# Hymba trunk layer on eight cores: order of loads and of the q, k, v projections at the start of the program

## The reference, cut to what matters

```python
h    = RMSNorm_pre(x)
p    = h @ W_in + b_in            # (16384, 2048) @ (2048, 5376)
q, k, v, g_attn, glu_val, glu_gate, g_conv = split(p)
attn = SlidingWindowGQA_with_sinks(partial_rope(q), partial_rope(k), v) * silu(g_attn)
conv = ConformerConv(glu_val, glu_gate) * silu(g_conv)
x    = x + RMSNorm_post(concat([attn, conv]) @ W_out + b_out)
```

## Time and profile before

| | us |
|---|---|
| median of 3 runs | 1105.92 (1105.06 to 1109.22) |
| the profiled execution | 1108.99 |
| its span, slowest core (core 2) | 1107.5 |
| spans of all cores | 1089.4 to 1107.5 |
| PE busy, core 2 | 1034.8 (93%) |
| DVE, ACT, POOL busy | 531.1 (48%), 412.2 (37%), 212.8 (19%) |
| DMA moved, core 2 | 141.92 MB |

### The profile page before, as it was taken

The page is one execution under the profiler, slowest core; times in us unless marked ns, Lnnn a source line. Parts: engine busy times, 40 slices in busy tenths (PEclk is TensorE's granted clock), DMA queues, the critical chain, the costliest instruction groups (busy, mean ns, idle before and its releaser), DMA issues.

```text
span 1107.5 us, 17820 instructions; the slowest of 8 cores (1089.4 to 1107.5 us)
## 1 busy us (share of the span) xinstructions
PE 1034.8 (93%) x6848; PEld 543.7 (49%) x6906; DVE 531.1 (48%) x921; ACT 412.2 (37%) x1013; POOL 212.8 (19%) x215
## 2 busy tenths in 40 slices
PE   3799999899999999999999999989999999999996
PEld 1556444555555444445544644455655544444443
DVE  3566301466665355446636650045776636533434
ACT  2452112556555445034511212155565544402111
POOL 0260000134543320000000000012455341000000
PEclk9899999999999999999999999999999999999999
DMA  8874334655566589979499303344645657992445
GB/s 184 277 113 79 57 48 76 127 116 117 128 136 131 147 191 159 192 200 204 91 171 185 78 10 67 76 102 108 177 122 140 152 141 174 165 180 41 81 76 109
DMA packets 26533, 141.92 MB, mean 128 GB/s; under 512 B 5985, under 2 KB 6369, under 8 KB 15969
## 3 DMA queue, kind: packets, MB, share of 16 engines
q0 software_dynamic: 8784, 80.74, 43.1%
q1 hardware_dynamic: 17666, 60.04, 17.7%
HBM read 171.72 MB, written 32.51 MB: 184 GB/s over the span
## 4 chain that ended last, share of the span: by engine, by line
PE 73%; DMA 7%; SPq 6%; DVE 6%; ACT 3%; issue 3%; POOL 1%; ACTq 0%; DVEq 0%; POOLq 0%
PE psum L1144 19%; PE psum L775 10%; PE psum L1023 10%; SPq L152 6%; DMA arena<-arena 5%; PE psum L635 5%; PE psum L1113 5%; PE psum L869 4%; PE psum L818 4%; PE psum L828 4%; PE psum L631 3%; PE psum L593 2%; ACT arena L928 2%; PE psum L530 1%; PE psum L1182 1%
## 5 line engine op out<-in xcount | busy, mean ns | idle before, releaser
L1144 PE MATMUL psum<-arena 128*128 128x512 bf16 x939 | 207.2, 379 | 1.1
L1144 PEld LDWEIGHTS psum<-arena 128*128 128x128 bf16 x960 | 93.6, 98 | 111.3
L818 PE MATMUL psum<-arena 128*128 128x352 bf16 (+1 forms) x768 | 124.3, 316 | 0.0
L828 PE MATMUL psum<-arena 128*128 128x352 bf16 (+1 forms) x768 | 120.9, 311 | 3.4 <-ACT arena L831 3.3
L928 ACT ACTIVATE arena<-psum,arena 128x128 f32<-128x128 f32 x256 | 93.9, 367 | 61.4 <-DVE arena L918 43.6
L1023 PE MATMUL psum<-arena 128*128 128x512 bf16 x500 | 110.9, 379 | 4.3 <-ACT arena L1027 3.0
L775 PE MATMUL psum<-arena 128*128 128x512 bf16 x502 | 113.6, 387 | 0.5
L828 PEld LDWEIGHTS psum<-arena 128*128 128x128 bf16 x768 | 74.8, 98 | 42.9 <-issue 5.3
L818 PEld LDWEIGHTS psum<-arena 128*128 128x128 bf16 x768 | 72.5, 99 | 47.6 <-issue 12.7
L907 DVE COPY_PREDICATED psum<-arena,psum 128x1024 f32<-128x1024 uint16 x32 | 38.7, 1208 | 117.7 <-PE psum L901 117.7
L942 POOL TENSOR_TENSOR arena<-arena 128x1024 bf16<-128x1024 f32 x32 | 60.5, 1892 | 140.7 <-DVE arena L941 140.7
(11 more groups left out here) (129 smaller groups left out, 1282.9 us busy)
## 6 DMA issues: line engine op xcount, KB each, us to landing
arena<-w_in POOLq DMA_DIRECT2D x12, 2048.0 KB, 16.0
arena<-x_ext SPq DMA_DIRECT2D x18, 1024.0 KB, 10.6
arena<-w_in POOLq DMA_DIRECT2D x16, 1024.0 KB, 10.4
out<-arena POOLq DMA_DIRECT2D x15, 1024.0 KB, 9.2
arena<-w_out POOLq DMA_DIRECT2D x6, 2048.0 KB, 20.2
arena<-arena SPq DMA_DIRECT2D x64, 66.0 KB, 2.0
arena<-arena SPq DMA_DIRECT2D x64, 65.9 KB, 2.0
arena<-arena SPq DMA_DIRECT2D x64, 65.9 KB, 2.3
```

Of the source, the lines that this page charges most:

```text
L818: cx.op('pe', lambda e, k=k: e.matmul(out=bank[bv][:, 0:n], lhsT=wbuf.ap[:, k, o:o + 128], rhs=xv[:, k, st:st + n], start=(k == 0), stop=( ...
L828: cx.op('pe', lambda e, k=k: e.matmul(out=bank[bg][:, 0:n], lhsT=wbuf.ap[:, k, o + 128:o + 256], rhs=xv[:, k, st:st + n], start=(k == 0), ...
L1144: cx.op('pe', lambda e, k=k: e.matmul(out=bank[b], lhsT=MIX.ap[:, k, j * 128:(j + 1) * 128], rhs=wo[n][k][0].ap[:, wo[n][k][1], :], start= ...
```

## The change

The program's first part is reordered; no arithmetic is changed.

- SP loads x tiles 0, 1, 2, the k/v bias and x tile 3 without a wait. POOL waits for x tile 1, then loads the k/v weights in two halves of 0.5 MB (as written) and the four quarters of q. x tile 4 waits for the second k/v half, tiles 5 to 7 for q's second, third and fourth quarter and for their buffer.
- The rotary tables are computed on DVE ahead of the copies of the norm's weights; the two sines on ACT come behind `p1_sq` of tile 2. A root is taken on ACT at the very start.
- Tiles 0 to 3 are projected by weight: k/v of all four, then q's first half (QA), then its second half (QB). Tiles 4 to 7 are projected tile by tile, k/v and q; tile 8, k/v alone.
- A product waits for the half of the transposed tile that it reads. k's rotation has scratch buffers of its own.

```diff
--- before.py
+++ after.py
@@ -367,6 +367,7 @@
         s_kvw = cx.dsem("kvw")
+        s_kvw2 = cx.dsem("kvw2")
...
@@ -410,7 +411,7 @@
-        rr_u = mk(O_CV + 2048, [NTIL, 8], F32)
+        rr_us = [mk(O_CV + o_, [NTIL, 8], F32) for o_ in (2048, 5120)]
...
             for which in range(2):
+                rr_u = rr_us[which]
...
-                cx.op('act', lambda e, which=which: e.activation(
+
+        def rope_sin():
+            for which in range(2):
+                rr_u = rr_us[which]
+                cx.op('act', lambda e, which=which, rr_u=rr_u: e.activation(
                     out=cs.ap[:, :, which * 8:(which + 1) * 8], in_=rr_u.ap, func=AF.Sin,
...
+            def xh(j, k):
+                return xts[j].a if k < 8 else xts[j].b
...
+            rk1 = [at([2, 2, 8], F32) for _ in range(2)]
+            rk2 = [at([2, 2, 8], F32) for _ in range(2)]
...
+                kvh = [mk(O_Z + 4096 * h, [8, 256], BF16) for h in range(2)]
...
-                kf, kb, r1, r2 = kvf[n % 3], kb2[n % 3], rt1[n % 2], rt2[n % 2]
+                kf, kb, r1, r2 = kvf[n % 3], kb2[n % 3], rk1[n % 2], rk2[n % 2]
...
-                        start=(k == 0), stop=(k == 15)), R=[KVW, xts[j]], W=[BK[b]])
+                        start=(k == 0), stop=(k == 15)), R=[kvh[k // 8], xh(j, k)], W=[BK[b]])
...
@@ -668,86 +682,87 @@
             if s == 0:
                 bufs = p1_bufs(0)
                 gp = bufs[2]
-                order = [1, 2, 3, 4, 5, 6, 7, 8, 0]
                 grow = mk(O_AT, [D], F32)
                 wslot["n"] = 1
                 wq0 = [[mk(O_WB + h * 8192 + q * 4096, [8, 256], BF16) for q in range(2)] for h in range(2)]
+                wq0f = wq0[0] + wq0[1]
                 cx.dma('sp', grow.ap[0:1, :], gpre_d[0:1, :], s_gpre, W=[grow], nowait=True)
                 cx.dma('sp', pos_i.ap, pos_t, s_c2, W=[pos_i], nowait=True)
                 cx.dma('sp', cpa.ap, cpack_d[:, 0:NCA], s_c, W=[cpa], nowait=True)
-                p1_load(0, order[0], 0, bufs)
+                order = [1, 2, 3, 4, 5, 6, 7, 8, 0]
+                for n in range(3):
+                    p1_load(0, order[n], n, bufs)
+                cx.dma('sp', bkv.ap, bqkv_d[:, 1024:1280], s_bkv, W=[bkv])
+                p1_load(0, order[3], 3, bufs)
+                for h, sem in ((0, s_kvw), (1, s_kvw2)):
+                    cx.dma('pool', kvh[h].ap, wv(w_in, 1024, 256, 8 * h, 8), sem, R=[bufs[0][1]], W=[kvh[h]])
                 for i in range(4):
-                    cx.dma('pool', wq0[i // 2][i % 2].ap, wv(w_in, 256 * (i // 2), 256, 8 * (i % 2), 8), s_wq[i],
-                           R=[cpa], W=[wq0[i // 2][i % 2]])
-                p1_load(0, order[1], 1, bufs, R=[wq0[0][0]])
-                cx.dma('sp', bq.ap, bqkv_d[:, 0:1024], s_bqkv, R=[wq0[0][1]], W=[bq])
-                p1_load(0, order[2], 2, bufs)
-                p1_load(0, order[3], 3, bufs, R=[wq0[1][0]])
-                p1_load(0, order[4], 4, bufs, R=[wq0[1][1]])
-                cx.dma('sp', cpb_.ap, cpack_d[:, NCA:NCP], s_c3, W=[cpb_])
-                cx.dma('sp', bkv.ap, bqkv_d[:, 1024:1280], s_bkv, W=[bkv])
+                    cx.dma('pool', wq0f[i].ap, wv(w_in, 256 * (i // 2), 256, 8 * (i % 2), 8), s_wq[i], W=[wq0f[i]])
+                p1_load(0, order[4], 4, bufs, R=[kvh[1]])
+                cx.dma('sp', bq.ap, bqkv_d[:, 0:1024], s_bqkv, W=[bq])
                 onesr = mk(O_AT + 8192, [128], F32)
                 cx.op('dve', lambda e: e.memset(onesr.ap, 1.0), W=[onesr])
+                cx.op('act', lambda e: e.activation(out=smp[3].ap[:, 0:1], in_=onesr.ap[:, 0:1], func=AF.Sqrt),
+                      R=[onesr], W=[smp[3]])
                 cx.op('dve', lambda e: e.tensor_copy(out=idn.ap, in_=cp[:, C_ID:C_ID + 128]), R=[cpa], W=[idn])
                 gpq = [mk(gp.off + n * 2048, [512], F32) for n in range(4)]
                 for n in range(4):
                     cx.op('pe', lambda e, n=n: e.matmul(
                         out=bank[n], lhsT=onesr.ap[0:1, :], rhs=grow.ap[0:1, n * 512:(n + 1) * 512],
                         start=True, stop=True), R=[onesr, grow], W=[BK[n]])
+                rope_tables()
+                for n in range(4):
                     cx.op('dve', lambda e, n=n: e.tensor_copy(
                         out=gpq[n].ap, in_=bank[n]), R=[BK[n]], W=[gpq[n]])
-                rot["i"] = 4
+                rot["list"] = [0, 1, 2, 3]
+                rot["i"] = 0
                 junk = mk(O_AT + 12288, [D], BF16)
-                xns = {}
-                rope_tables()
-
-                def qstep(n, done=None):
-                    j = order[n]
-                    b_ = q_a(0, j, wq0, done, 'pool')
-                    return lambda: q_b(0, j, b_)
-
-                p1_sq(0, order[0], 0, bufs, junk)
-                xns[0] = p1_n(0, order[0], 0, bufs)
-                p1_b(0, order[0], xns[0])
-                p1_sq(0, order[1], 1, bufs, junk)
-                xns[1] = p1_n(0, order[1], 1, bufs)
-                b0, b1 = nbank(), nbank()
-                q_h(b0, order[0], wq0, 0)
-                p1_b(0, order[1], xns[1])
-                p1_sq(0, order[2], 2, bufs, junk)
-                for n in (5, 6):
-                    p1_load(0, order[n], n, bufs)
-                q_h(b1, order[1], wq0, 0)
-                q_h(b0, order[0], wq0, 1)
-                f0 = qstep(0, b0)
-                xns[2] = p1_n(0, order[2], 2, bufs)
-                p1_sq(0, order[3], 3, bufs, junk)
-                later(f0)
-                q_h(b1, order[1], wq0, 1)
-                f1 = qstep(1, b1)
-                p1_b(0, order[2], xns[2])
-                xns[3] = p1_n(0, order[3], 3, bufs)
-                p1_load(0, order[7], 7, bufs)
-                p1_load(0, order[8], 8, bufs)
-                p1_sq(0, order[4], 4, bufs, junk)
-                later(f1)
-                for n in range(2, 9):
-                    if n + 1 < 9:
-                        p1_b(0, order[n + 1], xns[n + 1])
-                    if n + 2 < 9:
-                        xns[n + 2] = p1_n(0, order[n + 2], n + 2, bufs)
-                    fq = qstep(n) if order[n] > 0 else None
-                    if n + 3 < 9:
-                        p1_sq(0, order[n + 3], n + 3, bufs, junk)
-                    if fq:
-                        later(fq)
-                    if n == 3:
-                        cx.dma('pool', KVW.ap, wv(w_in, 1024, 256), s_kvw, W=[KVW])
-                        wq1 = wload(w_in, 512)
+                xns, kvs, qs = {}, {}, {}
+
+                def SQ(n):
+                    p1_sq(0, order[n], n, bufs, junk)
+
+                def N(n):
+                    xns[n] = p1_n(0, order[n], n, bufs)
+                    if n + 5 < 9:
+                        p1_load(0, order[n + 5], n + 5, bufs, R=[wq0f[n + 1]] if n < 3 else ())
+
+                def B(n):
+                    p1_b(0, order[n], xns[n])
+
+                def KV(n):
+                    kvs[n] = kv_a(order[n])
+
+                def KT(n):
+                    kv_b(order[n], kvs[n])
+
+                def QA(n):
+                    q_h(4 + n, order[n], wq0, 0)
+
+                def QB(n):
+                    q_h(4 + n, order[n], wq0, 1)
+                    qs[n] = q_a(0, order[n], wq0, 4 + n, 'pool')
+
+                def QQ(n):
+                    qs[n] = q_a(0, order[n], wq0, None, 'pool')
+
+                def QT(n):
+                    q_b(0, order[n], qs[n])
+
+                SQ(0), N(0), B(0), SQ(1), N(1), B(1), SQ(2), rope_sin(), N(2)
+                KV(0), B(2), SQ(3), N(3), KV(1), KT(0), B(3), KV(2), KT(1), KV(3), KT(2)
+                QA(0), QA(1), QA(2), QA(3), KT(3), SQ(4), N(4)
+                QB(0), B(4), KV(4), QB(1), SQ(5), N(5), B(5), QT(0), QB(2), KT(4), KV(5)
+                QT(1), QB(3), SQ(6), N(6), B(6), QT(2)
+                rot["list"] = list(range(8))
+                QQ(4), KT(5), KV(6), SQ(7), N(7), B(7), QT(3)
+                cx.dma('sp', cpb_.ap, cpack_d[:, NCA:NCP], s_c3, W=[cpb_])
+                wq1 = wload(w_in, 512)
+                QQ(5), KT(6), KV(7), SQ(8), N(8), B(8), QT(4)
+                QQ(6), KT(7), KV(8), QT(5), QQ(7), KT(8)
                 late_consts()
-                for jj in order:
-                    kb = kv_a(jj)
-                    later(lambda jj=jj, kb=kb: kv_b(jj, kb))
+                later(lambda: QT(6))
+                later(lambda: QT(7))
             else:
                 wq0, wq1 = nxt["wq"]
                 for j in range(1, 9):
```

More of the change, by code:

```diff
@@ L425, in rope_tables @@
             for which in range(2):
+                rr_u = rr_us[which]
                 shift = 0.25 if which == 0 else 0.0
                 lo, hi = (-1.5 * PI, 0.5 * PI) if which == 0 else (-PI, PI)
-                cx.op('dve', lambda e, shift=shift: e.tensor_scalar(
+                cx.op('dve', lambda e, shift=shift, rr_u=rr_u: e.tensor_scalar(
                     out=rr_u.ap, in0=ang.ap, scalar1=float(1.0 / (2 * np.pi)), scalar2=shift,
```

(26 more changed lines are left out.)

## The result

The change made the kernel slower: 1134.28 us median of 4 runs (1133.77 to 1136.49) against 1105.49 before (1102.23 to 1109.22), ratio 1.0263 with a 95% interval of 1.0228 to 1.0299. The profiled execution's slowest core, core 5, has a span of 1132.2 us.

What follows compares the result with a forecast made beforehand. PE bounds the kernel, so its arrival at q's last 512 columns decides: 51 + 36.0 + 27.5 + 10.5 = 125.0 us against 98.6, 26.4 later, taking the median from 1105.9 to 1132; range 1112 to 1141.

Steps and rivals of the forecast that it cites:

- When QB of tile 0 starts: Start of q's second half on tile 0, first product needing q's last weight quarter: 51 us, ends 45.5 and 57.
- The DMA limit: Landing of q's last weight quarter: 45.5 us, or 48.9 if x tile 5 is served between.
- the second limit: PE's order from k/v weights at about 27 us, through tile 3's transposes at 38.7, to q's second half: 50 to 57.
- PE's work: From q's second half on tile 0 to the first product of q's last 512 columns: 36.0 us, no waits, full clock.
- The waits that the change adds: PE standing still for the norm ahead of the transposes of tiles 4 to 8: 27.5 us in sum, lower end 23.6.
- The clock: Granted clock falling after each of five new waits: 2.1 us each, 10.5 in all; ends none and 17.
- Edits at nothing: x halves as wait, k's own scratch, early root, rope tables first, late last q weights: no effect on the time.
- The clock stays up: Rival: the waits stand but the clock does not fall; 114.5 us at q's last 512 columns, time 1122; chance 0.21.
- The early start wins: Rival: norms of tiles 4 to 8 ready when PE asks; q's last 512 columns at 87.0, time 1094; chance 0.07.
- It evens out: Rival: q's second half at 45.5, waits half as long (13.7), no clock loss; time 1103 to 1108; chance 0.06.
- worse: Rival: half clock until 57 us and the full 17 us of clock loss; time 1145; chance 0.04.
- The join's starting point: First product of q's last 512 columns in the kernel before, read at 98.56 us; the forecast moved it 26.4 later.

Runs made afterwards that it cites:

- the run with filled waits: The changed kernel plus products of 512 columns that nobody reads, placed in PE's five waits for a norm: 1124.95 us, ratio 1.0185.
- The old kernel with the norm late: The kernel before the change, with only the norm of tiles 4 to 8 called directly ahead of each tile's transposes: 1123.45 us, ratio 1.0187.
- the norms ahead: The changed kernel with square and norm of tiles 4 to 8 called one step earlier, loads and products as in the change: 1102.05 us, ratio 0.9987.
- the better order: The changed kernel's loads and projection by weight, with every square and norm at least one step ahead and q's last weights asked for earlier: 1098.54 us, ratio 0.9958.

## Why the prediction was right

Sign, size and mechanism came out: 1132 forecast, 1134.28 measured. Some terms came out in the sum and not one by one. Term by term on core 5:

- **When QB of tile 0 starts**: 51 taken from ends of 45.5 and 57; measured 51.08. The DMA limit was nearer to its lower end: the last quarter landed at 45.5 and not at 48.9, so x tile 5, issued at 34.62, was not served ahead of it: it landed at 47.8. The order on PE set the start, as the second limit had it: k/v weights at about 27 (the products start at 23.81 with the first half and at 26.91 with the second), tile 3 transposed at 37.67 for 38.7. That 51 was hit so closely is luck in part. It was chosen between two ends, and two errors of 1 and 2 us offset each other: tile 3's transposes came 1.0 early, and from them to QB it took 13.4 us where 11.4 were counted (a k/v product at half clock, 3.36 for 1.91, and k's transposes, which the sum leaves out).
- **PE's work**: 36.0 us. With the five waits of 27.26 taken off, 126.07 - 51.08 leaves 47.7; the run with filled waits puts 9.7 of that on the clock on this core. The rest, 2 us over the sum, has the wait of 0.40 at 59.00 and the ends of the groups ahead of a wait: the spacing counts a group to the start of the next, which is 0.16 us less than its own length.
- **The waits that the change adds**: 3.9, 4.9, 5.3, 6.7 and 6.7 forecast; 3.75, 4.75, 5.36, 6.70 and 6.70 measured, and the chain inside them is the one that was written down.
- **The clock**: 2.1 us for each wait, 10.5; the filled run shows 9.5, 1.9 for each in the mean. The sum was right and the even share was not: single waits cost 1.6 to 2.7 us on core 5. The Trainium skill's "TensorE: Matmul & The Clock Gate", section "HAM oscillation", has the clock lost anew in every pass with a wait. The change's trace agrees for its five waits on core 5. The old kernel with the norm late does not for all: behind one of five waits of 3.33 us the q product took 3.62. An estimate by the page's example, 4 us, would have been less than half of what the join gained when the waits were filled; the row of before was the better source.
- **Edits at nothing**: held in their sum. The first norm, forecast some 4 us later for the rope tables, came 7.9 us earlier (12.61 on core 5, 20.49 on core 2 of before), with x tile 0 there sooner (squared from 10.08 and from 16.70); nothing rested on it. The weights of q's last columns were not late in the change. When the waits went, they were, by 0.44 to 2.58 us.

*The clock stays up* fell: 0.67 in the windows from 80 to 100 us. *The early start wins* was right in its mechanism and wrong in its condition: with the norms ahead the join came at 95.0 and, in the better order, at 91.35, but not at 87. *It evens out* and *worse* had no part. The join's starting point was read too late: core 2, on which the rows of before were read, was the latest of eight at the join (98.56 against a median of 95.8), so the move by the medians is 30.2 us and by that row 27.5. Of the 3.8 us that the forecast of 26.4 was short of the median move, 2.8 are that choice of core and 1.1 the join itself (126.07 for 125.0). The time's 28.8 lies between.

## What to carry to other kernels

Where each engine keeps the order of the code, the distance between a producer's call and its consumer's is the prefetch: read each new neighbourhood on the waited engine and add the chain of all engines between two neighbours. A stage must be called before the work that its engine would otherwise wait for, and not so early that it stands ahead of what PE needs sooner. A wait of 3 to 7 us on PE cost its length and, in these kernels, 0 to 2.7 us more for the clock.

## What the runs showed of the hardware

Useless work can make a kernel faster: 112 products of 512 columns, in waits that stayed as long, brought the join from 126.0 to 116.5. The price per wait did not hang on its length: two waits of 6.70 us cost 2.7 and 1.6 us, and of five waits of 3.33 us four cost about 1.7 each on core 1 and one nothing. Also, the granted clock reads 1.00 from the start of the profile, while the 16 transposes at 22.99 take 1.86 us instead of 1.06. The window of the kernel before, core 2:

```profile
22.00:24.00 2.00, 1.01 (x10) 1.04 (x11) 0.84 (x1) 0.00 (x0) 0.00 (x0) 1.00 1.07 270
```

At the start of a profile the durations tell the clock's level, and the column does not.
